# Attention and state stage of a fused encoder layer: interleaved scores, feature-major value matmul, state groups in pairs, another form of the decay

## What is computed

```python
# attention; a chunk is 64 positions, a band is this chunk and the one before
scores = einsum('bclkgd,bcmkd->bckglm', q, k_band) * HEAD_DIM ** -0.5
m = maximum(max(scores, axis=-1), sink)
p = exp(scores - m)
probs = p / (sum(p, axis=-1) + exp(sink - m))
o = einsum('bckglm,bcmkd->bclkgd', probs, v_band)
# state mixer
decay = exp(where(causal, a_cs[l] - a_cs[s], -inf))
w = einsum('bclgn,bcsgn->bclsg', cm, bm)[..., None] * decay * dt
y_diag = einsum('bclsgh,bcsghp->bclghp', w, xs)
chunk_states = einsum('bcsgn,bcsgh,bcsghp->bcghpn', bm, decay_to_end * dt, xs)
# carry: state = state * chunk_decay + chunk_states
y_off = einsum('bclgn,bcghpn,bclgh->bclghp', cm, prev_state, exp(a_cs))
y = y_diag + y_off + d * xs
```

## Time and profile before

| | |
|---|---|
| time, median of 3 runs | 1539.64 us (1538.91 to 1540.72) |
| span of the profiled execution | 1529.4 us |
| PE busy | 1469.6 us, 96% of the span |
| DVE, ACT, POOL busy | 789.6, 498.1, 475.8 us |
| DMA, mean over the span | 139 GB/s |

### The profile page before, as it was taken

How to read it: one execution, slowest core, us unless ns; L and a number is a source line. 1 busy time by engine, 2 the same in 40 slices (tenths; PEclk the granted TensorE clock), 3 DMA queues, 4 the chain that set the end, 5 groups by cost and what they waited for, 6 DMA issues and landing times.

```text
span 1529.4 us, 22063 instructions
## 1 busy us (share of the span) xinstructions
PE 1469.6 (96%) x7744; PEld 1173.8 (77%) x7744; DVE 789.6 (52%) x977; ACT 498.1 (33%) x766; POOL 475.8 (31%) x238
## 2 busy tenths in 40 slices
PE   5999999999999998999999999999999999999999
PEld 4878888888888877777777777777777888787787
DVE  5369665444453014556565676657565554465411
ACT  6242222333322214233332424242416653332200
POOL 1122122122121232323324242332324766533321
PEclk8999999999999998999999999999999999999999
DMA  5213222222222266667666676766566636434422
GB/s 206 69 49 112 80 82 83 109 82 96 96 88 105 96 172 129 162 139 184 159 180 156 183 172 146 182 136 191 133 212 232 220 129 215 167 126 159 152 85 79
DMA packets 150328, 212.42 MB, mean 139 GB/s; under 512 B 6320, under 2 KB 111024, under 8 KB 150304
## 3 DMA queue, kind: packets, MB, share of 16 engines
q1 hardware_dynamic: 127888, 163.60, 37.8%
q10 hardware_dynamic: 20144, 39.98, 7.0%
q0 software_dynamic: 2272, 8.52, 1.4%
HBM read 150.87 MB, written 61.21 MB: 139 GB/s over the span
## 4 chain that ended last, share of the span: by engine, by line
PE 62%; issue 14%; DMA 10%; DVE 6%; POOL 4%; ACT 2%; SPq 1%; DVEq 0%; POOLq 0%; ACTq 0%
PE F L151 50%; DMA sb_early<-z_d 4%; DMA sb_acc<-cs_d 3%; PE F L1325 3%; PE M L1325 3%; DVE sb_early L815 2%; DMA y_d<-sb_acc 2%; POOL sb_whl L161 2%; POOL sb_res L1149 1%; SPq L633 1%; PE F L724 1%; PE F L721 1%; PE M L557 1%; POOL sb_early L970 1%; DMA g_d<-sb_res 1%
## 5 line engine op out<-in xcount | busy, mean ns | idle before, releaser
L151 PE MATMUL F<-sb_X,sb_whl 128*128 128x512 f32 x4800 | 1163.9, 402 | 7.8 <-POOL sb_whl L161 3.5
L151 PEld LDWEIGHTS F<-sb_X,sb_whl 128*128 128x128 f32 x4800 | 906.7, 190 | 245.5 <-issue 25.8
L161 POOL TENSOR_TENSOR sb_whl<-sb_wst,sb_whl 128x1024 fp32r<-128x1024 f32 x109 | 272.5, 2500 | 799.8 <-ACT sb_whl L158 799.4
L158 ACT ACTIVATE sb_whl<-sb_wst 128x1024 fp32r<-128x1024 f32 x109 | 115.1, 1056 | 259.6 <-PE F L151 117.0
L815 DVE TENSOR_SCALAR sb_early<-sb_acc,sb_ssd_sb 128x128 f32<-128x128 f32 x256 | 101.7, 472 | 11.4 <-DMA sb_acc<-cs_d 11.4
L925 ACT ACTIVATE sb_res<-F 128x512 f32<-128x512 f32 x64 | 38.2, 598 | 194.7 <-PE F L151 191.5
L477 DVE TENSOR_SCALAR sb_early<-F,sb_acc 128x1024 f32<-128x1024 f32 x24 | 30.8, 1284 | 134.7 <-PE F L151 134.7
L479 DVE SCALAR_TENSOR_TENSOR sb_early<-F,sb_acc,sb_early 128x1023 f32<-128x1023 f32 (+2 forms) x72 | 92.3, 1282 | 10.5 <-DVE sb_early L477 0.2
L794 DVE TENSOR_SCALAR M<-M,sb_cst 64x256 f32<-64x256 f32 x32 | 15.5, 483 | 156.8 <-PE M L656 156.8
L441 DVE TENSOR_TENSOR sb_early<-sb_early 32x1024 f32<-32x1024 f32 x40 | 63.3, 1581 | 30.4 <-ACT sb_early L339 29.8
L1213 DVE SCALAR_TENSOR_TENSOR sb_X<-sb_X,sb_cst x16 | 54.6, 3413 | 35.8 <-POOL sb_part L1136 35.8
(11 more groups left out here) (148 smaller groups left out, 1234.4 us busy)
## 6 DMA issues: line engine op xcount, KB each, us to landing
sb_wst<-w_units SPq DMA_DIRECT2D x109, 512.0 KB, 3.5
sb_acc<-cs_d SPq DMA_DIRECT2D x8, 2048.0 KB, 22.2
x_d<-sb_res ACTq DMA_DIRECT2D x24, 512.0 KB, 2.7
z_d<-sb_res ACTq DMA_DIRECT2D x24, 512.0 KB, 2.8
sb_early<-x_d SPq DMA_DIRECT2D x8, 1024.0 KB, 8.1
sb_acc<-ecs_d SPq DMA_DIRECT2D x16, 512.0 KB, 32.2
g_d<-sb_res ACTq DMA_DIRECT2D x16, 512.0 KB, 6.6
y_d<-sb_acc POOLq DMA_DIRECT2D x8, 1024.0 KB, 15.1
```

Source lines behind the costliest of these rows:

```text
L151: last = nc.tensor.matmul(bank, whl[:, slot, wp, k, :], act[:, ap, k, half * HALF:(half + 1) * HALF], start=(k == 0 and wp == 0 and ap == ...
L158: return nc.scalar.activation(whl[:, slot, 0], wst[:, slot], ACT.Copy)
L161: return nc.gpsimd.tensor_tensor(whl[:, slot, 1], wst[:, slot], whl[:, slot, 0].bitcast(f32), ALU.subtract)
```

## The change

- `scores` issues both row halves of the array in turn: for each c it goes over u = 0, 1 and both output halves, so that four 64x64 tiles follow one another; before, the four c of one u came first.
- The probabilities are divided by their sum on DVE before they are transposed (`normalise`), and `attend` takes v as the fixed operand, so that its output has features on partitions. `o_T` and `o_rows` go.
- Probabilities have four buffers instead of two.
- Decay: instead of 32 subtractions with a minimum on DVE, DVE takes `min(csb, cs)` for a group at once, in place (`causal`, 128x1024), and ACT does the subtraction as the bias of the exponential, 8 of 128x128 per group. `ncs_sb` holds the negated sums, made once.
- The state groups go in pairs: diagonal parts of two, state parts of two, new states of two, then half units; the pair uses two banks of O and two of Tb. `y_out` is split into `y_take` and `y_out`.
- The order of work on every engine is written anew. Among it: SP issues v earlier, `csb` ahead of `bc`, and z ahead of `ecsb`; `csb`'s release is the last decay of the iteration before; `x_dt(0)`, `x_dt(1)`, `causal(0)` and `causal(1)` stand between the first and the second pair of `maxima`; the store of y goes from POOL's queue to ACT's.

The core of the diff:

```diff
             def scores(r0):
-                u = r % 2
                 for c in range(4):
-                    for half in range(2):
-                        last = nc.tensor.matmul(S[64 * half:64 * half + 64, u, c * P:(c + 1) * P],
-                                                qs[64 * u:64 * u + 64, 4 * (r // 2) + c, 64 * half:64 * half + 64],
-                                                ks[64 * u:64 * u + 64, r // 2, 64 * half:64 * half + P], start=True, stop=True)
-                last.then_inc(sc_done, 1)
+                    for u in range(2):
+                        for half in range(2):
+                            last = nc.tensor.matmul(S[64 * half:64 * half + 64, u, c * P:(c + 1) * P],
+                                                    qs[64 * u:64 * u + 64, 2 * r0 + c, 64 * half:64 * half + 64],
+                                                    ks[64 * u:64 * u + 64, r0 // 2, 64 * half:64 * half + P], start=True, stop=True)
+                last.then_inc(sc_done, 2)
...
+                to = O[:, r // 2, :].rearrange("p (r a l) -> p r a l", r=2, a=2)
+                for half in range(2):
+                    at_l = slice(64 * half, 64 * half + 64)
+                    for u in range(2):
+                        last = nc.tensor.matmul(to[64 * u:64 * u + 64, r % 2, :, at_l], vs[:, half, r * HD:(r + 1) * HD],
+                                                pT_heads[:, r % 2, u, :, at_l], start=True, stop=True)
...
-            def seg(g):
...
-                for h in range(HG):
-                    last = nc.vector.tensor_scalar(dec[:, g % 2, h, :], csb[:, HG * g + h, :],
-                                                   cs_sb[:, ds(j, 1), HG * g + h:HG * g + h + 1].rearrange("p a h -> p (a h)"),
-                                                   0.0, ALU.subtract, ALU.min)
+            def normalise(b):
+                h8 = slice(8 * b, 8 * b + 8)
+                dve.wait_ge(sinke_ready, at(2, b + 1))
+                ch.link(nc.vector.tensor_tensor(stat[:, 3, h8], stat[:, 3, h8], stat[:, 2, h8], ALU.add))
+                ch.link(nc.vector.reciprocal(stat[:, 4, h8], stat[:, 3, h8]))
+                for r in (2 * b, 2 * b + 1):
+                    inv = stat[:, 4, 4 * r:4 * r + 4].unsqueeze(2).to_broadcast([P, 4, P])
+                    nc.vector.tensor_tensor(probs[:, r], probs[:, r], inv, ALU.mult).then_inc(norm_ready, 1)
+            def causal(g):
+                to = csb[:, HG * g:HG * g + HG, :]
+                nc.vector.tensor_tensor(to, to, per_head(cs_sb, HG * g, HG, P), ALU.min).then_inc(seg_ready, 1)
...
             def decay(g):
-                act.wait_ge(seg_ready, at(4, g + 2))
-                nc.scalar.activation(dec[:, g % 2], dec[:, g % 2], ACT.Exp).then_inc(dec_ready, 1)
+                act.wait_ge(seg_ready, at(4, g + 1))
+                for h in range(HG):
+                    last = nc.scalar.activation(dec[:, g % 2, h, :], csb[:, HG * g + h, :], ACT.Exp,
+                                                bias=ncs_sb[:, ds(j, 1), HG * g + h:HG * g + h + 1].rearrange("p a h -> p (a h)"))
+                last.then_inc(dec_ready, 1)
```

More of the change, by code:

```diff
@@ L762, in _ @@
                 x_rows(3)
-                b_rows_and_cb()
-                half_unit(3)
-                o_T(0)
-                o_T(1)
-                group(0)
-                half_unit(4)
-                group(1)
+                half_unit(4)
+                pe.wait_ge(oT_ready, at(2, 4))
+                pe.wait_ge(xdt_ready, at(4, 4))
+                diag(0)
+                diag(1)
+                off(0)
+                off(1)
+                pe.wait_ge(brow_ready, at(1, 1))
+                pe.wait_ge(cbm_ready, at(1, 1))
+                new_state(0)
+                new_state(1)
                 half_unit(5)
-                group(2)
                 half_unit(6)
-                group(3)
+                pe.wait_ge(y_taken, at(4, 3))
+                diag(2)
+                diag(3)
+                off(2)
+                off(3)
+                pe.wait_ge(state_ready, at(4, 3))
+                new_state(2)
+                new_state(3)
                 half_unit(7)
@@ L854, in add_state @@
                     nc.vector.tensor_tensor(state[:, g, :], state[:, g, :], S[:, g % 2, :], ALU.add).then_inc(state_ready, 1)
+                dve.wait_ge(sc_done, at(4, 3))
                 maxima(0)
                 maxima(1)
+                sink_shift(0)
                 x_dt(0)
                 x_dt(1)
+                dve.wait_ge(cs_in, at(16, 16))
+                causal(0)
+                causal(1)
+                dve.wait_ge(sc_done, at(4, 5))
                 maxima(2)
                 maxima(3)
[L862 to L873 removed]
+                sink_shift(1)
+                normalise(0)
+                normalise(1)
                 dve.wait_ge(cb_done, at(1, 1))
@@ L879, in _ @@
                 weights_T(1)
+                x_dt(2)
+                x_dt(3)
+                causal(2)
+                causal(3)
+                dve.wait_ge(z_in, at(16, 16))
                 o_out(0)
                 o_out(1)
-                for g in range(GROUPS):
-                    y_out(g)
-                    if g + 2 < GROUPS:
-                        seg(g + 2)
-                    add_state(g)
-                    if g + 2 < GROUPS:
-                        weights_T(g + 2)
+                dve.wait_ge(xd_ready, at(4, 5))
+                dve.wait_ge(ecs_in, at(32, 32))
+                dve.wait_ge(yg_done, at(4, 3))
+                y_take(1)
+                y_take(0)
+                add_state(0)
+                add_state(1)
+                weights_T(2)
+                weights_T(3)
+                dve.wait_ge(y_taken, at(4, 3))
+                y_out(1)
+                y_out(0)
+                dve.wait_ge(yg_done, at(4, 5))
+                dve.wait_ge(yout_ready, at(4, 3))
+                y_take(3)
+                y_take(2)
+                add_state(2)
+                add_state(3)
+                dve.wait_ge(y_taken, at(4, 5))
+                y_out(3)
+                y_out(2)
         @block.scalar
@@ L941, in _ @@
[L941 removed]
+                act.wait_ge(brt_done, at(1, 1))
+                nc.scalar.activation(flat(brow[:]), S[:, 0, :], ACT.Copy).then_inc(brow_ready, 1)
+                unit_out(0)
+                decay(0)
+                take_half(2)
+                act.wait_ge(pv_done, at(2, 2))
                 probs_out(2)
                 probs_out(3)
[L944 removed]
                 decay(1)
[L946 to L947 removed]
```

237 lines of the change are left out of this document (98 added, 139 removed).

## The result

The changed kernel takes 1498.8 us, the median of 4 runs (1494.9 to 1501.2), where the kernel before, run beside it, takes 1539.8: a ratio of 0.973, 95% interval 0.971 to 0.974. A second time it was 1496.3 against 1535.5, 0.974 (0.972 to 0.976).

What follows compares the result with a forecast made beforehand. PE, busy nearly the whole span, was taken as the bound. Iterations go from 72.5 to 69.8 us, 19 less over seven: 1529.4 - 19 = 1510.4, plus 10.2 around the span, 1520.6 us; range 1509 to 1538.

Steps and rivals of the forecast that it cites:

- the 10.2 around the span: Outside the profiled span: 10.2 us by which the median of the runs exceeds it, added to 1510.4.
- 17.1 + 52.7 = 69.8: One iteration: PE resumes at the probabilities' transposes at 17.1, then works 52.7; 69.8 us where it was 72.5.
- Groups in pairs hold the same matmuls in another order: zero.: PE's work at the state groups: pairing them changes only the order of matmuls, 0 us.
- 69.1 - 0.97 - 1.2: PE's work per iteration: 69.1 before, less 0.97 for `o_T` and 1.2 for interleaved scores, gives 66.9 us.
- I take 0.6 a place, 1.2 an iteration: PE's two score places per iteration: interleaving saves 0.6 of 1.52 us each, between bounds of nothing and 0.76.
- this wait is 1.9: PE ahead of `scores(2)`, waiting for ACT's exponentials: 1.9 us an iteration where 0.80 stood.
- So it waits 1.0: PE at the transposes of the probabilities, waiting for `normalise`: there at 16.1, goes on at 17.1, 1.0 us.
- `csb` lands at 8.6: DMA of the decay sums: lands 21 us after issue, 25.8 after half unit 5, so 8.6 into the next iteration.
- The slower rival: `csb` lands 26 us from issue, so PE goes on at 22.1 and an iteration takes 74.8: 1556 us; chance 0.12.
- So the waits of 18.0 in total go: PE ahead of the groups' diagonal parts: the 18.0 us of waits for DVE go, save for a little.
- This hides the gain of the scores whole: Waits at the exponentials (first place) and the probabilities' transposes (second) absorb the interleaving's gain; without it the forecast stays 1520.6.
- the first rival: `csb` lands 18 to 20 us from issue, PE isn't held: 68.8 an iteration, 1511 to 1514, down to 1509; chance 0.22.

Runs made afterwards that it cites:

- the kernel without the chain from `csb`: Changed kernel with DVE's `normalise(0)` directly behind `x_dt`, and `causal(0)`, `causal(1)` only behind the other two maxima: 1490.1 us, ratio 0.970.
- either one alone: Changed kernel with `normalise(0)` ahead of `causal(0)`, `causal(1)`: 1490.1 us; or with ACT's table load ahead of its wait for maxima: 1495.9 us; both edits: 1484.1 us.

## Why the prediction missed

The terms by which the forecast of 1520.6 was 21.8 too high are: 8.4 in what lies around the span (10.2 put, 1.8 measured), 17.4 in the spans (36.4 less, 19 forecast); minus 3.9, by which the profiled execution after was faster than its median. 8.4 + 17.4 - 3.9 = 21.9.

1. **"1529.4 - 19 = 1510.4, and with the 10.2 around the span": wrong.** I took the difference between one execution's span and other executions' times for a property of the program. Times are 1.6 to 1.9 above their own span. The profiled execution of before was a fast one of its kind: over the 40 runs of it in this case the kernel takes 1527 to 1541. Where its slower executions spend the 8 us is open, since the one trace of it shows a fast one. Without this error the forecast would have been 1512, and still too high.
2. **"The iteration is 17.1 + 52.7 = 69.8": 2.15 too long, 15.0 over seven.** Without its waits the iteration has 67.38 - 1.74 = 65.6 of work (the kernel without the chain from `csb`), where I had 66.9, and 1.74 + 0.26 = 2.0 of waits where I had 1.9 + 1.0.
   - Work: "Groups in pairs hold the same matmuls in another order: zero." It is 0.7 less, shown by the groups taken singly. This is the step of the mechanism that failed: I counted matmuls, and not the joints between kinds of them, that is the places where a run of one kind ends and the next begins.
   - Work: "PE's work in an iteration is then 69.1 - 0.97 - 1.2". The 69.1 was a mean that holds the falls of the clock. Iteration 6 of before has 71.43 less 2.7 of waits, 68.7. That is 0.4.
   - Work: "I take 0.6 a place, 1.2 an iteration": 0.49 a place, 1.0 in all. This error, 0.2, had the other sign. The Trainium skill, TensorEngine Tiling (Array Packing), Key Properties, says that tiles operate independently. By that the prediction had half, 0.76 a place; two thirds of it came.
   - Work: 68.7 - 0.97 - 0.98 - 0.7 = 66.05, so 0.4 is left. `attend`, which I put at zero, takes 1.08 in the rows of before and 1.03 after, twice, which is 0.1. For the rest the probabilities transposed eight in a row are a candidate; neither was tested alone, and the split is open.
   - Waits: "this wait is 1.9": 1.74. "So it waits 1.0" at `normalise`: 0.26. The chain's end was at 16.44, where I had 17.0: `maxima` and the shift took 3.46 for 3.6, the sum and reciprocal 0.43 for 0.65, the handovers less.
3. **"`csb` lands at 8.6": right, in part by luck.** From ACT's copy to the landing it is 25.2 where I had 25.8, and the rest of the iteration is 16.6 where I had 17.2; the two errors cancel. The price of a later one was right too: with `bc` ahead it lands 6.1 later and costs PE nearly 6 us of waiting an iteration, and 1.6 more by the clock. The slower rival, the same chain past its point, was a true one: one place later in SP's list makes the changed kernel slower than the old.
4. **"So the waits of 18.0 in total go": right**, and z was the cause of most: z ahead of `ecsb` alone takes them to 5.4. That one move gives 15 of the 41 us.
5. **"This hides the gain of the scores whole": right at the first place, half right at the second**, since the chain was not late enough to take all of it. Interleaving gives 0.2 an iteration in the changed kernel and nothing in the old. That it would give 0.5 once the chain is gone is worked out (67.86 - 0.49 = 67.37), and was not run.
6. **"Iteration 0 I leave as it is", "behind the stage nothing moves by more than 1 us"**: 1.3 and 1.8 less.
7. Two slips that change nothing above. "With `csb` between 20 and 22.4: 1514 to 1528": by the prediction's own 7 us for each us, 22.4 gives 1530. And "the minimum would gain nothing where POOL is quiet" doesn't hold: two `causal` take 2.35 us with POOL idle, the 16 subtractions of iteration 0 before, also with POOL idle, 3.23.

The range failed too. It closed at the first rival's lower end, which held the wrong 10.2, and it allowed nothing for a gain in the terms that I had set at zero.

## What to carry to other kernels

- Compare a time with the span of the same execution. A span of one execution against a median of others mixes what lies around a program with how its executions differ, and one trace can't tell these apart.
- Where PE is the bound, try small matmuls of a kind together: here 0.35 us for a pair of groups, nothing once, was over 5 us in the stage.
- When two chains end within 0.1 us, shorten both: either one alone gave 0 to 0.3 us an iteration here, both 1.24. A wait that vanishes from one place and stands with the same number at the next is the sign. Before PE is given less work, look at the DMA list for what comes last in it and is needed first.

## What the runs showed of the hardware

- A DVE operation of 128x4 with both inputs in SBUF took 1.51 us instead of 0.16 when it began 0.9 us into one of POOL's of 2.4 us; it ended with POOL's.
- Interleaving four 64x64 tiles took 32 score instructions from 1.52 to 1.03 us, in both kernels.
- PE was held by late weight loads without idle time in its matmul rows: 0.16 at one place showed only as 5.86 instead of 5.70 from a half unit's start to the next row.
- With the sums behind `bc`, where PE waits 5.1 to 7.1 us at `normalise`, the granted clock fell to its lower level for 6.8 us in each iteration, in iteration 6 from some 2 us into the wait (at 1037.3, where PE had been idle since 1035.2); where the longest wait was 1.74 us, it fell in none of seven iterations in the changed kernel, and in two of seven of one variant.
